# Weight stream of a two-block transformer kernel: two tiles to a transfer, two halves of the ring

## The reference

```
mod = silu(c) @ w_ada + b_ada                      # w_ada: 2048 x 12288, six gates and shifts
h = rmsnorm(x, g_mix) * (1 + sc1) + sh1
x = x + gt1 * hybrid_mixer(h, w_in, ...)           # pooling, 8-head attention, RG-LRU, then @ w_out
h = rmsnorm(x, g_ffn) * (1 + sc2) + sh2
x = x + gt2 * ((silu(conv(h @ w_gate)) * (h @ w_up)) @ w_down)      # d_ff = 5632
x = rmsnorm(x, final_g)
for l in range(2):                                 # second block, two layers
    u = rms_norm(x, norm_g[l]) @ w_in_2[l]         # four branches: sparse attention, retention,
    merged = sum(sigmoid(gate_n) * ((y_n * silu(z_n)) @ w_branch[n]))   # hgrn2, memory attention
    x = x + merged @ w_out_2[l]
```

## Time and profile before

| | us |
|---|---|
| runs of the kernel before | 3754.61 median of 3 (3748.34 to 3755.4) |
| the profiled execution, first to last instruction | 3754.2 |
| PE, DVE, ACT busy | 3245.3, 2041.5, 1479.0 |
| TensorE clock granted, mean | 0.913 of full speed |
| stream transfers, `w_raw<-w` | 1028 of 512 KB, median 3.3 us from issue to landing |
| `w_ada` transfers | 96 of 1024 KB, median 10.9 us |
| bytes moved | 653 MB, 174 GB/s over the span |

### The profile page before, as it was taken

How to read it: one execution, slowest core, us unless ns; L and a number is a source line. 1 busy time by engine, 2 the same in 40 slices (tenths; PEclk the granted TensorE clock), 3 DMA queues, 4 the chain that set the end, 5 groups by cost and what they waited for, 6 DMA issues and landing times.

```text
span 3754.2 us, 41586 instructions
## 1 busy us (share of the span) xinstructions
PE 3245.3 (86%) x14270; PEld 2677.7 (71%) x14270; DVE 2041.5 (54%) x1985; ACT 1479.0 (39%) x1658; POOL 55.8 (1%) x109
## 2 busy tenths in 40 slices
PE   4678886799999998597787899999888777999988
PEld 3566654688888887476676788887676666788877
DVE  6677626746565665445445455555354454455554
ACT  2232333344444544343342444443343333444433
POOL 1001000000000000000000000000000000000000
PEclk9778878899999999797898899999898898999999
DMA  9758713545555554152342355554343332455545
GB/s 373 317 235 334 294 62 150 209 168 190 183 192 189 184 190 162 62 186 73 119 167 84 122 192 192 193 190 157 119 146 116 120 123 90 157 193 193 192 160 179
DMA packets 163704, 653.02 MB, mean 174 GB/s; under 512 B 18353, under 2 KB 18513, under 8 KB 150561
## 3 DMA queue, kind: packets, MB, share of 16 engines
q1 hardware_dynamic: 148896, 547.03, 43.0%
q0 software_dynamic: 14720, 104.83, 7.0%
HBM read 649.69 MB, written 2.10 MB: 174 GB/s over the span
## 4 chain that ended last, share of the span: by engine, by line
PE 76%; DVE 11%; DMA 5%; issue 5%; ACT 3%; DVEq 0%; SPq 0%; POOLq 0%; ACTq 0%; POOL 0%
PE pg L700 23%; PE pg L702 23%; PE pg L701 23%; DMA R<-w_ada 3%; DVE R L1164 2%; DMA w_raw<-w 1%; PE pm L744 1%; PE pm L788 1%; PE pm L803 1%; PE pm L766 1%; PE pm L939 1%; ACT w_hi L392 1%; PE pm L999 1%; PE pm L886 1%; DVE w_lo L1045 0%
## 5 line engine op out<-in xcount | busy, mean ns | idle before, releaser
L1045 DVE TENSOR_TENSOR w_lo<-w_raw,w_hi 128x1024 fp32r<-128x1024 f32 x1028 | 1257.6, 1225 | 1300.0 <-ACT w_hi L392 1290.8
L392 ACT ACTIVATE w_hi<-w_raw 128x1024 fp32r<-128x1024 f32 x1028 | 1090.4, 1061 | 1784.8 <-PE pg L702 1609.6
L700 PE MATMUL pg<-w_hi,hT_hi 128*128 128x512 f32 x3488 | 1379.8, 396 | 84.7 <-DVE w_lo L1045 39.5
L701 PE MATMUL pg<-w_lo,hT_hi 128*128 128x512 f32 x3488 | 1372.2, 393 | 0.0
L702 PE MATMUL pg<-w_hi,hT_lo 128*128 128x512 f32 x3488 | 1371.2, 393 | 0.0
L700 PEld LDWEIGHTS pg<-w_hi,hT_hi 128*128 128x128 f32 x3488 | 665.3, 191 | 232.9 <-issue 76.9
L702 PEld LDWEIGHTS pg<-w_hi,hT_lo 128*128 128x128 f32 x3488 | 663.9, 190 | 140.7
L701 PEld LDWEIGHTS pg<-w_lo,hT_hi 128*128 128x128 f32 x3488 | 665.3, 191 | 138.2
L700 PE MATMUL pg<-w_hi,y_parts 128*128 128x512 f32 x608 | 237.5, 391 | 9.6 <-DVE y_parts L1064 9.6
L701 PE MATMUL pg<-w_lo,y_parts 128*128 128x512 f32 x608 | 237.2, 390 | 0.0
L702 PE MATMUL pg<-w_hi,y_parts 128*128 128x512 f32 x608 | 237.1, 390 | 0.0
(11 more groups left out here) (228 smaller groups left out, 1483.4 us busy)
## 6 DMA issues: line engine op xcount, KB each, us to landing
w_raw<-w SPq DMA_DIRECT2D x1028, 512.0 KB, 3.3
R<-w_ada POOLq DMA_DIRECT2D x96, 1024.0 KB, 10.9
R<-mem_T SPq DMA_DIRECT2D x1, 2048.0 KB, 18.1
x_rows<-x SPq DMA_DIRECT2D x1, 2048.0 KB, 24.6
out<-x_rows SPq DMA_DIRECT2D x1, 2048.0 KB, 6.3
con_sb<-con SPq DMA_DIRECT2D x1, 1472.0 KB, 6.7
small_w_sb<-small_w POOLq DMA_DIRECT2D x2, 576.0 KB, 3.7
R<-con POOLq DMA_DIRECT2D x1, 1024.0 KB, 5.2
```

What stands on the lines that cost most here:

```text
L392: act.activation(w_hi[:, g % RING, :, :].rearrange("p c n -> p (c n)"), raw[:, g % RING, :], ACT.Copy).then_inc(hi_done, 1)
L700: pe.matmul(out, hi, w_hi[:, slot, c, :], start=start, stop=False)
L701: pe.matmul(out, hi, w_lo[:, slot, c, :], start=False, stop=False)
L1045: tt(flat(w_lo[:, g % RING, :, :]), raw[:, g % RING, :], flat(w_hi[:, g % RING, :, :]).bitcast(F32), ALU.subtract).then_inc(lo_done, 1)
```

## The change

One transfer brings two tiles, 2g and 2g + 1, of 1024 KB into one half of the raw ring. SP waits until the second tile that stood in that half has been split (`+ 2` in place of `+ 1`, with g even). There is one semaphore for each half in place of one for each slot, and ACT waits for the half, so for both tiles, before it splits the first of them. The source of a pair is two pieces of 4 KB for each partition, 512 KB apart; the size of `raw`, the splits, the passes on PE and everything on POOL stay.

```
-        raw_in = [sem(f"raw_in{i}") for i in range(RING)]
+        raw_in = [sem(f"raw_in{i}") for i in range(RING // 2)]
...
-                for g in range(count):
+                for g in range(0, count, 2):
                     if not (first and g < RING):
 
-                        sp.wait_ge(lo_done, group * GT + g - RING + 1)
-                    sp.dma_start(raw[:, g % RING, :],
-                                 t["w"][bass.ds(group * GT + g, 1), :, :].rearrange("o p n -> (o p) n")
-                                 ).then_inc(raw_in[g % RING], 16)
+                        sp.wait_ge(lo_done, group * GT + g - RING + 2)
+                    sp.dma_start(raw[:, g % RING:g % RING + 2, :],
+                                 t["w"][bass.ds(group * GT + g, 2), :, :].rearrange("o p n -> p o n")
+                                 ).then_inc(raw_in[g % RING // 2], 16)
...
-                    act.wait_ge(raw_in[g % RING], 16 * (group * (GT // RING) + g // RING + 1))
+                    act.wait_ge(raw_in[g % RING // 2], 16 * (group * (GT // RING) + g // RING + 1))
```

## The result

| | before | with pairs |
|---|---|---|
| median of the runs, us | 3755.0 | 3798.6 (3793.8 to 3802.4, 4 runs) |
| profiled execution, span, us | 3754.2 | 3792.1 |
| ratio | | 1.0117 (1.0102 to 1.0131) |

What follows compares the result with a forecast made beforehand. The prediction took PE's three passes as most of the chain, with DVE the bound in the `w_ada` parts. It added 1.3 (start), 22 (`w_ada` parts) and 3 (first `w_out`), 26 us, for 3781 us, range 3762 to 3798.

Steps and rivals of the forecast that it cites:

- The mechanism: In the five parts of `w_ada`, pairs asked for later and useful only when whole stall DVE: +22 us (6 to 34).
- the start: At the program's first split, ACT must wait for the pair's second tile, at 31.62 instead of 30.34 us: +1.3 us.
- L: Beside a full `w_ada` queue, a pair's time from issue to landing: 9.5 us, or 10.5 with 1 us more.
- (L + 5.8)/2: In the `w_ada` parts, time for two steps, two ring halves taking turns: 7.7 to 8.15 us, taken as 7.8.
- that is no movement: In a pair's landing beside `w_ada`, the part of L besides moving bytes: about 2.0 us (3.3 less 1.27).
- The bounds: For the whole kernel, 3762 to 3798 us; the `w_ada` parts gave +6 at the low end and +34 at the high.
- The first pair of a part: In each `w_ada` part, tiles 4 and 5 land together and stall DVE 1.9 us, between 0 and 2.6.
- Beside the first `w_out`: While PE runs from 619.5 to 706.0 us, slower pairs and one late split cost +3 us (0 to 8).
- After 715 us: In feed-forward and layers, ACT's larger waits all end with PE, whose three split tiles cover a late pair: 0 us.
- The stream's share grows: Beside `w_ada`, engines serve longer runs of one transfer, so a pair lands in 7.0 us: 3757 to 3762, chance 0.20.
- Larger transfers move faster: In the `w_ada` parts, pairs lift the DMA rate and 33 long steps gain 0.37 us each: 3744 us, chance 0.04.
- More than the sum: In feed-forward and layers, late pairs also delay ACT, 100 groups at 0.5 us: 3830 us; above 3798, chance 0.05.

Runs made afterwards that it cites:

- the joint wait: Kernel before with single tiles, but ACT waits for both tiles of a half before splitting the even one: 3764.0 us against 3753.9, ratio 1.0028.
- the wide pieces: Kernel with pairs, the two tiles of a pair side by side in memory, so the stream comes in 8 KB pieces: 3771.6 us, ratio 1.0045.
- the thin `w_ada` with pairs against singles: Nearly all `w_ada` traffic cut in parts 0 to 4, in the kernel with pairs and the kernel before: pairs 3747.9 us, singles 3743.3 us.
- the turned order: Kernel with pairs, POOL asking for a `w_ada` chunk in parts 0 to 4 only after DVE's next split: 3790.7 us, ratio 1.0098.
- `w_ada` in 4 KB: Kernel with pairs, `w_ada` chunks fetched in pieces of 4 KB instead of 8 KB: 3771.0 us, ratio 1.0056.
- both pieces: Kernel with pairs, stream in pieces of 8 KB and `w_ada` in pieces of 4 KB: 3762.5 us, ratio 1.0021.
- the pairs that begin at the feed-forward: Kernel before with single tiles up to the feed-forward, pairs from the fifth tile of its first group on: 3754.3 us against 3753.5, ratio 1.0.

## Why the prediction was wrong

**The mechanism was right.** The five parts of `w_ada` carry 39 us in the profiled execution, every second split waits there, the chunks don't any more, the start costs 1.23 us (1.3 forecast), and the shift from the feed-forward on stays within 0.2 us between its first tile and the last.

**The step that failed is L, the landing of a pair beside a full `w_ada` queue.** The prediction took 7.8 us for two steps, which by its own (L + 5.8)/2 is L = 9.8; it was 12.1, and two steps took 8.99. The term that was too small is the one "that is no movement": 2.0 us were put for it, and about 2.5 us more pass before the pair's first piece moves (3.4 us after the issue instead of 1.0), while a chunk of `w_ada` goes ahead.

A sign of it stood in the earlier trace rows, but it could be read in two ways. The transfer issued at 118.8 had nothing of the stream ahead of it and still landed after 5.7 us, 2.4 more than alone. By the prediction's terms this is 2.0 us and one tile at a third of the speed (3.77 us), so nothing seemed to be missing. The records of the pieces say otherwise: its first piece moved after 3.2 us, behind 832 KB of `w_ada`, and then the whole tile moved within 2.1 us, nearly by itself. The 11.3 to 11.6 us of the single tiles were named too, and their excess put down to queueing behind other tiles. With 2.0 + 2.4 + 7.54 = 11.9 us the formula gives 8.9 us for two steps, 2.1 over DVE's pace, 10.5 us for five pairs and 8 us a part beyond what stood there: +40 in place of +22, and the sum 3798. This is worked out afterwards, and the third of the speed in it holds for the last engine only. That it meets the measured time so closely is luck in part: it counts 3 us beside the first `w_out`, of which the profiled execution shows 0.4.

**The bounds** were worked out from the same L, with 1 us for all that was not known: high 8.15 us for two steps, where 8.99 came. So the range ends at 3798, just below the measured time.

**The first pair of a part** was put at 1.9 us of stall; it had none in the second part. It landed in 6.8 us there: it waited for one chunk and then moved by itself, and the next chunk, issued at 129.1, moved only behind it. That is the low end that the prediction allowed ("if it were alone"). The first stall, 3.1 us (144.95 against 135.08 + 6.80), is the next pair's. The five stalls are 3.1, 1.9, 2.4, 1.0 and 3.5 us, 11.8 together. Why they scatter so is open.

**Beside the first `w_out`** 3 us were forecast and about 0.4 came in the profiled execution, where PE waits twice for a split, 2.0 us in all. This is no proof that PE's pace hides the rest: from tile 108 to 140 four other kernels lose 3.5 to 3.9 us in theirs (the joint wait, the wide pieces, the thin `w_ada` with pairs against singles, the turned order), two lose 0.6 and 0.7 (`w_ada` in 4 KB, both pieces). The 3 us may be right for most executions of the pairs; their other three runs have no trace.

**After 715 us** 0 was right, but not that ACT's waits all end with PE: 28 don't. PE's three split tiles cover it, as the text had it for the feed-forward alone.

**The rivals.** "The stream's share grows" supposed that a whole transfer takes its turn. The first pair of the second part did what it says (6.8 us to landing against its 7.0), the later ones did not, and that the time falls with the size of the pieces fits turns of one piece. "Larger transfers move faster" falls: the steps grew, and a pair that is alone lands 1.5 us after the time of a single tile (4.8 against 3.3), no less than the 1.27 us that a tile behind another adds. "More than the sum" by the later stages falls with the pairs that begin at the feed-forward.

**38 us in the profiled execution, 44 in the medians.** 2.8 of the 6 us are the clock in the attention (above). Without that the profiled difference is 41 us, and the interval of the ratio, 1.0102 to 1.0131, is 38 to 49 us, so no loss needs to be looked for elsewhere. The profiled run was also the shortest of its four. A part of the rest may be the 3 us beside the first `w_out`, which this execution did not show; no trace of the longer runs can tell.

## What to carry to other kernels

A double-sized transfer in a ring of the same size takes away twice: the first half is asked for later, and is of use later. Either may fit into the cover and both together not (+4 and +10 us alone, +44 together), so the time of one round (landing + work + next request) must be held against the pace of the consumer, with the landing taken from the most crowded stretch of the trace and not from the median of all: here 12 us against 4.8.

Where two queues load at once, the size of the contiguous pieces matters. Here wider pieces for the late stream or narrower ones for the other took the loss from +44 to +18 or +17 us, and both together to +7.5, without a byte more of buffer.

One profiled execution against another is not a measurement of a few microseconds: the same attention took 123 to 132 us by the clock that was granted. Compare the stretch that was changed, and the medians of many runs.

## What the runs showed of the hardware

- A transfer of 1024 KB beside a full queue of `w_ada` landed after 12.1, 9.4, 9.4 and 8.4 us (medians, 140 to 172 us) with pieces of 4 KB beside 8, 8 beside 8, 4 beside 4 and 8 beside 4; alone after 4.8 us.
- Two queues that were served in turn moved one piece each (133 of some 407 GB/s for pieces of 4 KB beside 8, 136.0 to 138.5 us), but whole transfers followed each other too: a chunk of 1024 KB, a pair of 1024 KB alone at 422 GB/s, the next chunk (126.5 to 135 us).
- The first piece of a transfer moved 1.0 us after the issue when the engines were free and 3.4 us after it (median) beside the other queue; with the order of the two requests turned round, 2.3 us.
- Nine tenths of a pair had moved after 6.6 us and the last piece after 10.5 us (issued at 158.4), so the landing told of the last engine and not of the mean.
- Two source pieces of a partition 512 KB apart or side by side made no difference to a lone transfer: 4.8 us to landing either way.
- TensorE's granted clock in one stretch of the same attention was 0.74, 0.73, 0.71 or 0.69 in the mean of different executions, and the stretch took 123, 126, 128 to 129 or 132 us.
